# FFN down projection: four pairs of contraction chunks as seven block products, with weight sums made by accumulating DMAs

## The chip, the core and the metric

One core of a Trainium2 chip runs the whole program. The metric is the device time of one execution in microseconds (us), lower is better. Before the change it is 2257.29 us, the median of 3 runs (2256.53 to 2257.57).

## The reference, cut to what matters

Two blocks of two layers each work on x of 256 tokens by 1024 channels in fp32. Every layer has two feed-forward stages (FFN) with a mixing stage between them, so there are eight FFNs:

```python
D_MODEL, SEQ, D_FF, DEPTH = 1024, 256, 2816, 2

def swiglu(h, w1, w3, w2):
    return (jax.nn.silu(h @ w1) * (h @ w3)) @ w2

h = rmsnorm(x, g_ffn1[l])
x = x + 0.5 * swiglu(h, w1_a[l], w3_a[l], w2_a[l])
...
h = rmsnorm(x, g_ffn2[l])
x = x + 0.5 * swiglu(h, w1_b[l], w3_b[l], w2_b[l])
```

The change is in the last product of each FFN, `( ... ) @ w2`: 256 x 2816 times 2816 x 1024.

## The kernel before, in words

**Products.** Each fp32 product is made of three matmuls: every operand is split into a rounded part ("hi", fp32r) and the rest ("lo"), and hi·hi, hi·lo and lo·hi are added in PSUM. Weights come in units of 128 x 2048 elements (1 MB). SP loads a unit in two DMAs into a ring `raw` of RAW = 3 buffers; ACT rounds it into `whi` (`split`, L1176); DVE subtracts to get `wlo` (`split`, L1646) and raises `w_ready`; PE uses both and raises `w_used`. `whi` and `wlo` have HL = 4 slots, so ACT may split unit u once PE is done with unit u - 4, and SP may load unit u once `w_ready` of unit u - 3 is there. All engines run in the order of the program text, and semaphores tie them together.

**One FFN.** It has FC = 22 hidden blocks of 128 channels (b = 0 to 21), one unit each, with gate and up weights side by side. For block b PE runs 16 matmuls of 512 columns and 16 of 256 (`hidden_chunks`, L666 and L667; in the very first FFN `hidden_high` and `hidden_low`, L677 and L685) into one of three pairs of PSUM banks. ACT then copies a part out (`low_parts`, L1242), DVE adds and scales (L1775, L1780), ACT applies silu (L1248), DVE multiplies (`hid`, L1785), ACT rounds `ht_hi` (L1253), and DVE makes `ht_lo` (L1791). In the same round DVE splits unit b + 3 and ACT splits unit b + 4.

**The down projection.** The 22 chunks of 128 hidden channels are the contraction; the result has two token tiles (m = 0, 1) and two halves of 512 channels. Before, 12 units per FFN are used: for half 0 five units of four chunks and one of two, then the same for half 1. `blocks` (L602 to L604) runs, for each chunk and each m, three matmuls of 128x512. After half 0 DVE adds its two PSUM banks to x with the factor `rhalf` (`add_to_x`, L1690), PE transposes that half of x for the next stage (`x_transposes`, L634) early in half 1, ACT and DVE turn it into the next stage's operand (L1188, L1661).

POOL does nothing before but four instructions at the start.

Of the kernel before, what the change touches and what calls it, by code (L numbers as in the profile page):

```python
# [27 lines left out]
P = 128  # L28
T = 256
# [9 lines left out]
SPACER = 40  # L39
RAW = 3  # L40
HL = 4

LAYERS = 2
FFN_UNITS = 2 * FG + 12
# [7 lines left out]
for b in (1, 2):  # L52
    for u in (0, FFN_UNITS + MIX_UNITS[b]):
        SHORT[b].update({u + FFN_UNITS - 7: 1024, u + FFN_UNITS - 1: 1024})
UNITS_BEFORE = {1: 0, 2: LAYERS * LAYER_UNITS[1]}
TOTAL_UNITS = LAYERS * (LAYER_UNITS[1] + LAYER_UNITS[2])
assert all(n % HL == 0 for n in LAYER_UNITS.values())
# [38 lines left out]
class Engine:  # L96
# [50 lines left out]

    def layer(self):

        return {1: 0, 2: LAYERS, "end": 2 * LAYERS}[self.block] + self.lay  # L150

# [24 lines left out]
def build(nc, a, known):  # L176
# [13 lines left out]
    with ctx:  # L190
# [19 lines left out]
        rhalf = sb(ctx, "rhalf", [P, MT])  # L210
        fss = sb(ctx, "fss", [P, 2, 2, MT])
# [32 lines left out]
        junk = sb(ffn, "junk", [P, MT, D])  # L244
        junk2 = sb(ffn, "junk2", [P, MT, D])
        gfin = sb(ffn, "gfin", [P, D])
        xgf = sb(ffn, "xgf", [P, MT, D])
# [116 lines left out]
        stored = semaphore("stored")  # L364

# [10 lines left out]
        def loaded(e, u):  # L376

            return 32 * (e.unit(u) // RAW + 1) - 16
# [28 lines left out]

        block = ctx.enter_context(nc.Block())
# [3 lines left out]
        def _(eng):  # L412
# [5 lines left out]
            def load(u, halves):  # L418

                r = e.unit(u) % RAW  # L420
                eng.wait_ge(w_ready, units(e, u))
                for dst, src in halves:
                    eng.dma_start(dst(raw[:, r, :]), src).then_inc(raw_in[r], 16)
# [29 lines left out]
            def ffn_loads(u0, gate_up_w, w2):  # L453
# [8 lines left out]
                for half in range(2):  # L462
                    for i in range(6):
                        plain(w2, FF, 4 * P * i, 512 * half, u0 + 2 * FG + 6 * half + i, 4 if i < 5 else 2)
# [80 lines left out]
            for _ in e.layers(1):  # L545
                ffn_loads(0, a["t_gate_up_1a"], a["w2_a"])
# [6 lines left out]
                ffn_loads(FFN_UNITS + MIX_UNITS[1], a["t_gate_up_1b"], a["w2_b"])  # L553
            for _ in e.layers(2):
                ffn_loads(0, a["t_gate_up_2a"], a["ffn1_w_down_2"])
# [7 lines left out]
                ffn_loads(FFN_UNITS + MIX_UNITS[2], a["t_gate_up_2b"], a["ffn2_w_down_2"])  # L563
# [15 lines left out]
        def _(eng):  # L579
# [7 lines left out]
            def blocks(u, block, p, split, chunks, start, stop, used, cols=512, beside=False, ready=True):  # L587
# [4 lines left out]
                slot = u % HL  # L592
                if block == 0 and ready:
                    eng.wait_ge(w_ready, units(e, u, RAW))
                for i, c in enumerate(chunks):
                    w = slice((block + i) * cols, (block + i + 1) * cols)
                    out = w if beside else slice(0, cols)
                    first = start and (beside or i == 0)
                    final = stop and (beside or i == len(chunks) - 1)
                    for m in range(MT):  # L600
                        t = slice(m * P, (m + 1) * P)
                        nc.tensor.matmul(pair(p, m)[:, out], hi[:, c, t], whi[:, slot, w], start=first, stop=False)  # L602
# [6 lines left out]
            def last_blocks(u, p, split, chunks):  # L609

                hi, lo = split
                slot = u % HL
# [45 lines left out]
            def hidden_chunks(u, p, chunks):  # L658

                slot = u % HL  # L660
# [11 lines left out]
            def hidden_high(u, p, chunks):  # L672

                for c in chunks:
                    for j in range(2):
                        first = 256 * c + P * j
                        nc.tensor.matmul(pair(p, j), whi[:, u % HL, first:first + P], xt[:, c, :, :], start=c == 0,  # L677
                                         stop=False)

            def hidden_low(u, p, chunks):  # L680

                for c in chunks:
                    for j in range(2):
                        first = 256 * c + P * j
                        last = nc.tensor.matmul(pair(p, j)[:, 0:T], wlo[:, u % HL, first:first + P], xt_hi[:, c, :],  # L685
# [4 lines left out]
            def ffn_tensor(u0, f, next_stage):  # L690
# [76 lines left out]

                u = u0 + 2 * FG
# [5 lines left out]
                blocks(u + 5, 0, 2, HT, (20, 21), False, True, True)  # L774

                u += 6
                blocks(u, 0, 1, HT, (0, 1), True, False, False)
# [3 lines left out]
                blocks(u, 2, 1, HT, (2, 3), False, False, True)  # L781
                for i in range(1, 5):
                    blocks(u + i, 0, 1, HT, range(4 * i, 4 * i + 4), False, False, True)
                if next_stage == "end":
                    last_blocks(u + 5, 1, HT, (20, 21))
                else:
                    blocks(u + 5, 0, 1, HT, (20, 21), False, True, True)
# [377 lines left out]
        def _(eng):  # L1165
            e = Engine(eng, counts, known, act_own)

            def split(u):
# [3 lines left out]
                r = e.unit(u) % RAW  # L1172
# [3 lines left out]
                nc.scalar.activation(whi[:, u % HL, 0:n], raw[:, r, 0:n], ACT.Copy).then_inc(hi_done, 1)  # L1176
# [58 lines left out]
            def ffn_scalar(u0, f, next_stage):  # L1235
                stage = f"ffn{f}"

# [12 lines left out]
                def hidden_hi(b):  # L1250

                    eng.wait_ge(hid_done, ffn_blocks(e, f, b))
                    nc.scalar.activation(ht_hi[:, b, :], hid[:, b % 2, :], ACT.Copy).then_inc(ht_hi_done, 1)  # L1253

# [39 lines left out]
                for b in range(2, FC):  # L1294
# [6 lines left out]
                    split(u0 + b + 4)  # L1301
                for s in range(2 * FG + 1, FFN_UNITS):
                    if s == 2 * FG + 6:
# [8 lines left out]
                    split(u0 + s + 3)  # L1312
# [321 lines left out]

        @block.vector
        def _(eng):
            e = Engine(eng, counts, known, dve_own)

            def split(u):
# [4 lines left out]
                r = e.unit(u) % RAW  # L1644
                n = SHORT.get(e.block, {}).get(u, 2048)
                nc.vector.tensor_tensor(wlo[:, u % HL, 0:n], raw[:, r, 0:n], whi[:, u % HL, 0:n],  # L1646
# [77 lines left out]
            def rstd_diag(stage):  # L1724

                nc.vector.memset(ones[:, :], 1.0)
                nc.vector.tensor_scalar(rhalf[:, :], rstd[:, :], 0.5, None, ALU.mult)
                for m in range(MT):
# [40 lines left out]
            def ffn_vector(u0, f, next_stage):  # L1769
                stage = f"ffn{f}"  # L1770

# [16 lines left out]
                def hidden_lo(b):  # L1788
# [3 lines left out]
                        ht_done, 1)  # L1792

# [41 lines left out]
                for b in range(2, FC):  # L1835
# [6 lines left out]
                    split(u0 + b + 3)  # L1842
                    hidden_lo(b)
                split(u0 + FC + 3)
                for s in range(2 * FG + 1, FFN_UNITS - 1):
                    if s == 2 * FG + 5:
                        multiplied(u0 + s)
# [571 lines left out]
```

## Time and profile before

| what | value |
|---|---|
| median of 3 runs | 2257.29 us |
| profiled execution, first to last instruction (span) | 2255.2 us |
| left around it, by the median | 2.1 us |
| PE busy | 2249.8 us, 100% |
| DVE busy | 1546.0 us, 69% |
| ACT busy | 1238.9 us, 55% |
| POOL busy | 0.2 us |
| mean granted TensorE clock | 1.000 |
| loaded by DMA | 417.61 MB, mean 185 GB/s |

The profile's times are of one execution. Busy time of PE is the union of its matmuls, which overlap (one of 512 columns lasts 0.39 us while the next starts after 0.23 us), so the cost of a matmul is the distance between two starts, not its length.

### The profile page before, as it was taken

The numbers are of one execution on the slowest core, as the hardware profiler recorded it, in microseconds if no ns is written. First come the engines' busy times: TensorE is split into PE (matmuls) and PEld (weight loads), VectorE is DVE, ScalarE is ACT, GpSimd is POOL, SyncE is SP. The second block draws the span as 40 slices with busy tenths as digits, with TensorE's granted clock in tenths as the row PEclk, the third lists the DMA queues.
The fourth block names the chain that finished last, engine by engine and source line by source line (L and its number), as shares of the span: only waits on it lengthen the run. The fifth ranks groups of instructions, "written<-read, shape, count | busy, mean of one in ns | idle before, by whom it ended". The sixth has DMA issues, their size and how long they took to land.

```text
span 2255.2 us, 28960 instructions
## 1 busy us (share of the span) xinstructions
PE 2249.8 (100%) x11686; PEld 1920.7 (85%) x11686; DVE 1546.0 (69%) x2179; ACT 1238.9 (55%) x1489; POOL 0.2 (0%) x4
## 2 busy tenths in 40 slices
PE   9999999999999999999999999999999999999999
PEld 8888888888888888888888888888888888888887
DVE  7764567765774566775776599767657747976773
ACT  7644445554653544654554576465555537755652
POOL 0000000000000000000000000000000000000000
PEclk9999999999999999999999999999999999999999
DMA  7556455555555455554555553545555555345553
GB/s 264 205 198 219 168 191 175 196 196 174 191 187 205 168 175 199 187 197 169 201 190 202 192 169 129 206 155 191 206 177 187 185 180 195 109 172 196 184 191 126
DMA packets 176213, 417.61 MB, mean 185 GB/s; under 512 B 16816, under 2 KB 20784, under 8 KB 176080
## 3 DMA queue, kind: packets, MB, share of 16 engines
q1 hardware_dynamic: 175936, 415.76, 53.3%
q8 instruction: 92, 1.51, 0.3%
q14 instruction: 41, 0.34, 0.0%
q10 hardware_dynamic: 144, 0.00, 0.0%
HBM read 414.66 MB, written 1.05 MB: 184 GB/s over the span
## 4 chain that ended last, share of the span: by engine, by line
PE 98%; DMA 1%; DVE 0%; SPq 0%; ACT 0%; issue 0%; DVEq 0%
PE psum L666 25%; PE psum L602 17%; PE psum L604 17%; PE psum L603 17%; PE psum L667 13%; PE psum L677 3%; PE psum L634 2%; PE psum L685 2%; PE psum L976 1%; DMA xt_in<-t_xt_dram 0%; PE psum L797 0%; DMA raw<-t_gate_up_1a_dram 0%; PE psum L954 0%; PE psum L817 0%; PE psum L944 0%; PE psum L966 0%
## 5 line engine op out<-in xcount | busy, mean ns | idle before, releaser
L1646 DVE TENSOR_TENSOR split_w<-raw,split_w 128x2048 fp32r<-128x2048 f32 (+1 forms) x405 | 881.1, 2182 | 285.8 <-ACT split_w L1176 284.9
L1176 ACT ACTIVATE split_w<-raw 128x2048 fp32r<-128x2048 f32 (+1 forms) x405 | 736.2, 1828 | 311.1 <-PE psum L604 288.2
L666 PE MATMUL psum<-xt,split_w 128*128 128x512 f32 x2464 | 859.2, 393 | 0.1
L667 PE MATMUL psum<-xt,split_w 128*128 128x256 f32 x2464 | 689.2, 280 | 0.0
L666 PEld LDWEIGHTS psum<-xt,split_w 128*128 128x128 f32 x2464 | 461.2, 187 | 104.3 <-DVE split_w L1646 1.3
L667 PEld LDWEIGHTS psum<-xt,split_w 128*128 128x128 f32 x2464 | 465.3, 189 | 0.3
L602 PE MATMUL psum<-split_w,xt 128*128 128x512 f32 (+1 forms) x736 | 289.5, 393 | 0.0
L604 PE MATMUL psum<-split_w,xt 128*128 128x512 f32 (+1 forms) x736 | 283.7, 385 | 0.0
L603 PE MATMUL psum<-split_w,xt 128*128 128x512 f32 (+1 forms) x736 | 283.6, 385 | 0.0
L602 PE MATMUL psum<-split_w,ht_hi 128*128 128x512 f32 x700 | 272.9, 390 | 0.0
L604 PE MATMUL psum<-split_w,ht_lo 128*128 128x512 f32 x700 | 272.5, 389 | 0.0
L603 PE MATMUL psum<-split_w,ht_hi 128*128 128x512 f32 x700 | 272.5, 389 | 0.0
L1775 DVE TENSOR_TENSOR gate<-psum,low 128x256 f32<-128x256 f32 x176 | 74.5, 423 | 155.3 <-ACT low L1242 155.1
L602 PEld LDWEIGHTS psum<-split_w,xt 128*128 128x128 f32 x736 | 138.4, 188 | 28.9 <-issue 3.0
L604 PEld LDWEIGHTS psum<-split_w,xt 128*128 128x128 f32 x736 | 138.2, 188 | 28.1
L1242 ACT ACTIVATE low<-psum 128x512 f32<-128x512 f32 x176 | 104.5, 594 | 103.7 <-PE psum L667 94.3
L603 PEld LDWEIGHTS psum<-split_w,xt 128*128 128x128 f32 x736 | 138.4, 188 | 25.6
L1248 ACT ACTIVATE gate<-gate 128x256 f32<-128x256 f32 x176 | 72.9, 418 | 158.4 <-DVE gate L1780 158.4
L604 PEld LDWEIGHTS psum<-split_w,ht_lo 128*128 128x128 f32 x700 | 131.4, 188 | 27.3
L602 PEld LDWEIGHTS psum<-split_w,ht_hi 128*128 128x128 f32 x700 | 131.4, 188 | 27.2
L603 PEld LDWEIGHTS psum<-split_w,ht_hi 128*128 128x128 f32 x700 | 131.4, 188 | 26.9
L1253 ACT ACTIVATE ht_hi<-hid 128x256 fp32r<-128x256 f32 x176 | 72.6, 417 | 91.4 <-DVE hid L1785 91.4
(278 smaller groups left out, 1951.2 us busy)
## 6 DMA issues: line engine op xcount, KB each, us to landing
raw<-w_in_dram SPq DMA_DIRECT2D x180, 512.0 KB, 4.4
raw<-t_gate_up_1b_dram SPq DMA_DIRECT2D x88, 512.0 KB, 4.1
raw<-t_gate_up_2a_dram SPq DMA_DIRECT2D x88, 512.0 KB, 4.1
raw<-t_gate_up_2b_dram SPq DMA_DIRECT2D x88, 512.0 KB, 4.1
raw<-t_gate_up_1a_dram SPq DMA_DIRECT2D x84, 512.0 KB, 4.1
raw<-ffn_w_down_dram SPq DMA_DIRECT2D x80, 512.0 KB, 4.2
raw<-w_a_dram SPq DMA_DIRECT2D x40, 512.0 KB, 4.4
raw<-w_b_dram SPq DMA_DIRECT2D x40, 512.0 KB, 4.4
```

The lines of the kernel that those rows point to most:

```text
L602: nc.tensor.matmul(pair(p, m)[:, out], hi[:, c, t], whi[:, slot, w], start=first, stop=False)
L603: nc.tensor.matmul(pair(p, m)[:, out], hi[:, c, t], wlo[:, slot, w], start=False, stop=False)
L604: last = nc.tensor.matmul(pair(p, m)[:, out], lo[:, c, t], whi[:, slot, w], start=False, stop=final)
L666: nc.tensor.matmul(bank, whi[:, slot, w], xt[:, c, :, :], start=c == 0, stop=False)
L667: last = nc.tensor.matmul(bank[:, 0:T], wlo[:, slot, w], xt_hi[:, c, :], start=False, stop=c == DC - 1)
L677: nc.tensor.matmul(pair(p, j), whi[:, u % HL, first:first + P], xt[:, c, :, :], start=c == 0, stop=False)
L1176: nc.scalar.activation(whi[:, u % HL, 0:n], raw[:, r, 0:n], ACT.Copy).then_inc(hi_done, 1)
L1242: nc.scalar.activation(low[:, b % 2, :, :], psum[:, first:first + 2, T:2 * T], ACT.Copy).then_inc(low_done, 1)
L1248: nc.scalar.activation(gate[:, b % 2, :], gate[:, b % 2, :], ACT.Silu).then_inc(gate_done, 1)
L1253: nc.scalar.activation(ht_hi[:, b, :], hid[:, b % 2, :], ACT.Copy).then_inc(ht_hi_done, 1)
L1646: nc.vector.tensor_tensor(wlo[:, u % HL, 0:n], raw[:, r, 0:n], whi[:, u % HL, 0:n], ALU.subtract).then_inc(w_ready, 1)
L1775: return nc.vector.tensor_tensor(out[:, b % 2, :], bank[:, 0:T], low[:, b % 2, j, :], ALU.add)
```

## The change: what it does

Of the 22 chunks, 14 stay as they are (`ALONE`). The other eight form four pairs (4, 5), (8, 9), (12, 13), (16, 17). For a pair the result is a 2 x 2 block product: two token tiles by two chunks, times two chunks by two halves. Before, that is 8 block products of 128x128 by 128x512; now it is 7, by a scheme in which some products take sums of activations and sums of weights. Each of the seven products is one unit that holds its four pairs: `11`, `21`, `22` are plain quarters of the weights, loaded through the ring, and `U`, `T3`, `T2`, `T4` are sums of quarters.

- **Weight sums.** Two buffers `added` hold them. SP loads quarter 11 into the first after unit 14 of the hidden blocks and quarter 12 into the second after unit 16. POOL then issues DMAs that add a quarter from DRAM to what the buffer holds: 12 onto the first (U), 22 onto the second (T3), and later, once U is split, 22 onto the first (T2), and once T2 is split, 21 onto the first (T4). Each sum is two DMAs of 512 KB. ACT's split of such a unit waits for its sum.
- **Activation sums.** After blocks 5, 9, 13 and 17 DVE makes four sums of the pair's activations (128x128 each), ACT rounds them (`sums_rounded`, 128x512) and DVE makes their rest (`sums_lo`).
- **PSUM.** Product 11 starts a bank that T2 and later T3 go on adding to; DVE adds this bank to x between (`part_to_x`, with `rhalf` or `minus_half`), and PE waits on `taken` before T2 and before T3. U has a bank of its own, and the bank pair it shares with 11 is that of hidden block 21. The other products go into the banks of the plain chunks.
- **Order.** The 15 units of the down projection run as `DOWN` lists them; the transposes of half 0 of x now come in the middle of unit 12 of 15.
- Buffers are renumbered (`place` counts only units that go through the ring), and `SPACER` goes from 40 to 32.

The core of the diff:

```diff
+QUARTERS = ("11", "21", "22")
+MIXED = range(4, 20, 4)
+ALONE = ((0, 1, 2, 3), (6, 7, 10, 11), (14, 15, 18, 19), (20, 21))
+DOWN = (("plain", 0, ALONE[0]), ("product", "U"), ("product", "11"), ("plain", 0, ALONE[1]), ("product", "21"),
+        ("plain", 0, ALONE[2]), ("product", "T2"), ("product", "22"), ("plain", 0, ALONE[3]), ("plain", 1, ALONE[0]),
+        ("product", "T4"), ("product", "T3"),
+        ("plain", 1, ALONE[1]), ("plain", 1, ALONE[2]), ("plain", 1, ALONE[3]))
+ADDED = {"U": (0, "12"), "T3": (1, "22"), "T2": (0, "22"), "T4": (0, "21")}
...
-FFN_UNITS = 2 * FG + 12
+FFN_UNITS = 2 * FG + len(DOWN)
...
             def ffn_loads(u0, f, gate_up_w, w2):
...
+                    if b == 14:
+                        eng.wait_ge(ht_done, ffn_blocks(e, f, 2))
+                        added_load(w2, 0, "11")
+                    if b == 16:
+                        added_load(w2, 1, "12")
...
+                def product(u, name):
+                    out, start, stop = OUT[name]
+                    resumed = name in ("T2", "T3")
+                    slot = e.unit(u) % HL
+                    eng.wait_ge(w_ready, units(e, u, RAW))
+                    for i in range(4):
+                        hi, lo = LEFT[name](i)
+                        w = slice(i * 512, (i + 1) * 512)
+                        nc.tensor.matmul(out, hi, whi[:, slot, w], start=start and i == 0, stop=False,
+                                         skip_group_check=resumed)
+                        nc.tensor.matmul(out, hi, wlo[:, slot, w], start=False, stop=False, skip_group_check=resumed)
+                        last = nc.tensor.matmul(out, lo, whi[:, slot, w], start=False, stop=stop and i == 3,
+                                                skip_group_check=resumed)
+                    last.then_inc(w_used, 1)
...
-                for i in range(5):
-                    blocks(u + i, 0, 2, HT, range(4 * i, 4 * i + 4), i == 0, False, True)
+                blocks(u, 0, 2, HT, ALONE[0], True, False, True)
+                eng.wait_ge(pair_free, ffn_blocks(e, f, FC - 1))
+                product(u + 1, "U")
+                product(u + 2, "11")
+                blocks(u + 3, 0, 2, HT, ALONE[1], False, False, True)
+                product(u + 4, "21")
+                blocks(u + 5, 0, 2, HT, ALONE[2], False, False, True)
+                eng.wait_ge(taken, 2 * ffns(e, f) + 1)
+                product(u + 6, "T2")
+                product(u + 7, "22")
                 eng.wait_ge(ht_done, ffn_blocks(e, f, FC - 1))
...
+                product(u + 10, "T4")
+                eng.wait_ge(taken, 2 * ffns(e, f) + 2)
+                product(u + 11, "T3")
...
+            def product_split(u, f, name):
+                if name in QUARTERS:
+                    split(u)
+                    return
+                eng.wait_ge(summed_in[name], 32 * (ffns(e, f) + 1))
+                eng.wait_ge(w_used, units(e, u))
+                nc.scalar.activation(whi[:, e.unit(u) % HL, :], added[:, ADDED[name][0], :], ACT.Copy).then_inc(hi_done, 1)
...
+                def sum_of(name):
+                    i, q = ADDED[name]
+                    for j in range(2):
+                        eng.dma_start(added[:, i, 1024 * j:1024 * j + 1024].rearrange("p (k n) -> p k n", k=2),
+                                      quarter(w2, e.lay, q)[:, 2 * j:2 * j + 2, :], accum_op=ALU.add
+                                      ).then_inc(summed_in[name], 16)
+                eng.wait_ge(added_in[0], 32 * n)
+                sum_of("U")
+                eng.wait_ge(added_in[1], 32 * n)
+                eng.wait_ge(summed_in["U"], 32 * n)
+                sum_of("T3")
+                eng.wait_ge(summed_in["T3"], 32 * n)
+                eng.wait_ge(w_ready, units(e, u + 1, RAW))
+                sum_of("T2")
+                eng.wait_ge(summed_in["T2"], 32 * n)
+                eng.wait_ge(w_ready, units(e, u + 6, RAW))
+                sum_of("T4")
...
+                def sums():
+                    both = hid.rearrange("p two (m t) -> p two m t", m=MT)
+                    e.link(nc.vector.tensor_tensor(sa[:, 0, :], both[:, 0, 1, :], both[:, 1, 1, :], ALU.subtract))
+                    nc.vector.tensor_tensor(sa[:, 1, :], both[:, 0, 0, :], both[:, 0, 1, :], ALU.subtract)
+                    e.link(nc.vector.tensor_tensor(sa[:, 2, :], sa[:, 0, :], both[:, 0, 0, :], ALU.subtract))
+                    nc.vector.tensor_tensor(sa[:, 3, :], sa[:, 2, :], both[:, 1, 0, :], ALU.add).then_inc(sums_done, 1)
```

How it moves instructions, at three places. On ACT, at the end of a round of the hidden blocks that closes a pair (here block 5 of the first FFN; `low` opens the round, and the last row splits a weight unit). The change has:

```order
L1362 ACTIVATE low<-psum 128x512 [waits w_used]
L1368 ACTIVATE gate<-gate 128x256 [waits scaled_done]
L1373 ACTIVATE ht_hi<-hid 128x256 [waits hid_done]
L1378 ACTIVATE sa_hi<-sa 128x512 [waits sums_done]
L1286 ACTIVATE split_w<-raw 128x2048 [waits w_used,raw_in1]
```

Before, the same round was `low`, `gate`, `ht_hi` and the split with nothing between. What is new is the row `sa_hi`, which waits for DVE's sums and stands ahead of the split.

On ACT, the splits of the down projection from its unit 3 on. Before:

```order
L1253 ACTIVATE ht_hi<-hid 128x256 [waits hid_done]
L1176 ACTIVATE split_w<-raw 128x2048 [waits w_used,raw_in1]
L1176 ACTIVATE split_w<-raw 128x2048 [waits w_used,raw_in2]
L1176 ACTIVATE split_w<-raw 128x1024 [waits w_used,raw_in0]
```

The change has (`added` is the buffer of sums, and `summed_in_T2` says that its DMAs landed):

```order
L1373 ACTIVATE ht_hi<-hid 128x256 [waits hid_done]
L1286 ACTIVATE split_w<-raw 128x2048 [waits w_used,raw_in0]
L1286 ACTIVATE split_w<-raw 128x2048 [waits w_used,raw_in1]
L1286 ACTIVATE split_w<-raw 128x2048 [waits w_used,raw_in2]
L1295 ACTIVATE split_w<-added 128x2048 [waits w_used,summed_in_T2]
L1286 ACTIVATE split_w<-raw 128x2048 [waits w_used,raw_in0]
L1286 ACTIVATE split_w<-raw 128x1024 [waits w_used,raw_in1]
L1286 ACTIVATE split_w<-raw 128x2048 [waits w_used,raw_in2]
L1295 ACTIVATE split_w<-added 128x2048 [waits w_used,summed_in_T4]
L1295 ACTIVATE split_w<-added 128x2048 [waits w_used,summed_in_T3]
```

The splits of T2, T4 and T3 stand in line with the others, so what is behind them on ACT waits for the sums too.

On DVE, the same stretch of the change (L2007 is `part_to_x`, which takes a bank out of PSUM; `hid` closes block 21):

```order
L1971 TENSOR_TENSOR hid<-up,gate 128x256 [waits gate_done,pair_free]
L1820 TENSOR_TENSOR split_w<-raw,split_w 128x2048 [waits hi_done]
L1977 TENSOR_TENSOR ht_lo<-hid,ht_hi 128x256 [waits ht_hi_done]
L1820 TENSOR_TENSOR split_w<-raw,split_w 128x2048 [waits hi_done] x3
L2007 SCALAR_TENSOR_TENSOR x<-psum,rhalf,x 128x512 [waits w_used]
L2007 SCALAR_TENSOR_TENSOR x<-psum,rhalf,x 128x512 x2
L1830 TENSOR_TENSOR split_w<-added,split_w 128x2048 [waits hi_done]
```

Before, DVE had only splits here until half 0 was complete. Now three `part_to_x` stand ahead of T2's split, which in turn releases POOL's DMAs for T4.

## Rows read from the trace of the kernel before

**Rows 1.** Page: span, busy time of the engines, and the last chain.
```profile
span 2255.2 us, 28960 instructions
PE 2249.8 (100%) x11686; PEld 1920.7 (85%) x11686; DVE 1546.0 (69%) x2179; ACT 1238.9 (55%) x1489; POOL 0.2 (0%) x4
...
PE 98%; DMA 1%; DVE 0%; SPq 0%; ACT 0%; issue 0%; DVEq 0%
```

**Rows 2.** Waits of PE over the whole span: us in total, times, longest.
```profile
PE psum L1153 <- DVE junk L2302: 1.3, 1, 1.3
PE psum L677 <- DVE xt L1677: 0.6, 1, 0.6
PE psum L677 <- ACT split_w L1176: 0.2, 1, 0.2
```

**Rows 3.** PE in order of time, first down projection: start us, length us.
```profile
130.35 0.40 PE L602 MATMUL psum<-split_w,ht_hi 128*128 128x512 f32 x1
...
135.81 0.39 PE L602 MATMUL psum<-split_w,ht_hi 128*128 128x512 f32 x1
...
163.02 1.03 PE L634 MATMUL psum<-ident,x 128*128 128x128 f32 x8
```

**Rows 4.** Groups by shape, 130 to 191 us: busy us, mean ns; idle before.
```profile
L1646 DVE TENSOR_TENSOR split_w<-raw,split_w 128x2048 fp32r<-128x2048 f32 x10 | 22.7, 2288 | 17.3 <-ACT split_w L1176 17.3
L1176 ACT ACTIVATE split_w<-raw 128x2048 fp32r<-128x2048 f32 x10 | 19.1, 1919 | 23.3 <-PE psum L604 23.3
L1646 DVE TENSOR_TENSOR split_w<-raw,split_w 128x1024 fp32r<-128x1024 f32 x2 | 2.5, 1226 | 4.1 <-ACT split_w L1176 4.1
L1690 DVE SCALAR_TENSOR_TENSOR x<-psum,rhalf,x 128x512 f32<-128x512 f32 x2 | 1.4, 748 | 3.9 <-PE psum L604 3.9
```

**Rows 5.** DVE in order of time, one round of the hidden blocks and the last split.
```profile
114.48 0.42 DVE L1775 TENSOR_TENSOR gate<-psum,low 128x256 f32<-128x256 f32 x1 [1.17 <-ACT low L1242]
114.94 0.42 DVE L1780 TENSOR_TENSOR gate<-gate,rstd_row 128x256 f32<-128x256 f32 x1
115.28 0.41 DVE L1775 TENSOR_TENSOR up<-psum,low 128x256 f32<-128x256 f32 x1
115.92 0.43 DVE L1785 TENSOR_TENSOR hid<-up,gate 128x256 f32<-128x256 f32 x1 [0.22 <-ACT gate L1248]
116.26 2.28 DVE L1646 TENSOR_TENSOR split_w<-raw,split_w 128x2048 fp32r<-128x2048 f32 x1
118.46 0.42 DVE L1791 TENSOR_TENSOR ht_lo<-hid,ht_hi 128x256 fp32r<-128x256 f32 x1
...
133.32 2.28 DVE L1646 TENSOR_TENSOR split_w<-raw,split_w 128x2048 fp32r<-128x2048 f32 x1
```

**Rows 6.** ACT in order of time: dense rounds early, then waiting ones.
```profile
45.89 0.58 ACT L1242 ACTIVATE low<-psum 128x512 f32<-128x512 f32 x1
50.53 0.57 ACT L1242 ACTIVATE low<-psum 128x512 f32<-128x512 f32 x1
...
113.85 0.60 ACT L1242 ACTIVATE low<-psum 128x512 f32<-128x512 f32 x1 [0.81 <-PE psum L685]
...
119.41 0.60 ACT L1242 ACTIVATE low<-psum 128x512 f32<-128x512 f32 x1 [0.81 <-PE psum L685]
...
130.55 0.60 ACT L1242 ACTIVATE low<-psum 128x512 f32<-128x512 f32 x1 [0.81 <-PE psum L685]
```

**Rows 7.** DMA, 130 to 191 us: queue (share), issues (KB, us to landing).
```profile
q1 hardware_dynamic: 7095, 13.81, 65.4%
raw<-w_a_dram SPq DMA_DIRECT2D x12, 512.0 KB, 4.5
```

**Rows 8.** DMA in 40 slices of 130 to 191 us: busy tenths, GB/s.
```profile
DMA  4960648999980039707920089997999992197149
GB/s 107 345 240 0 187 157 242 398 357 351 367 320 30 0 73 345 281 0 200 391 102 0 0 282 271 336 325 243 387 383 406 359 345 70 35 314 266 73 105 399
```

**Rows 9.** Clock over the whole span.
```profile
core 0: 2255.2 us, clock 1.000
```

More of the change, by code:

```diff
@@ L461, in ffn_loads @@
                                   ).then_inc(gfin_in, 16)
-                for half in range(2):
-                    for i in range(6):
-                        plain(w2, FF, 4 * P * i, 512 * half, u0 + 2 * FG + 6 * half + i, 4 if i < 5 else 2)
+                for i, part in enumerate(DOWN):
+                    if part[0] == "plain":
+                        _, half, chunks = part
+                        alone(w2, chunks, 512 * half, u0 + 2 * FG + i)
+                    elif part[1] in QUARTERS:
+                        rows = quarter(w2, e.lay, part[1])
+                        load(u0 + 2 * FG + i, [(chunked(1024 * j, 2, 512), rows[:, 2 * j:2 * j + 2, :]) for j in range(2)])
             def mix1_loads(u0):
@@ L676, in hidden_high @@
                         first = 256 * c + P * j
-                        nc.tensor.matmul(pair(p, j), whi[:, u % HL, first:first + P], xt[:, c, :, :], start=c == 0,
+                        nc.tensor.matmul(pair(p, j), whi[:, e.unit(u) % HL, first:first + P], xt[:, c, :, :], start=c == 0,
                                          stop=False)
@@ L684, in hidden_low @@
                         first = 256 * c + P * j
-                        last = nc.tensor.matmul(pair(p, j)[:, 0:T], wlo[:, u % HL, first:first + P], xt_hi[:, c, :],
+                        last = nc.tensor.matmul(pair(p, j)[:, 0:T], wlo[:, e.unit(u) % HL, first:first + P], xt_hi[:, c, :],
                                                 start=False, stop=c == DC - 1)
@@ L1236, in ffn_scalar @@
                 stage = f"ffn{f}"
+                second = range(MIXED.start + 1, MIXED.stop + 1, MIXED.step)
                 def low_parts(b):
@@ L1770, in ffn_vector @@
                 stage = f"ffn{f}"
+                second = range(MIXED.start + 1, MIXED.stop + 1, MIXED.step)
                 def summed(out, b, j):
@@ new lines, in ffn_vector @@
+                    if b in second:
+                        eng.wait_ge(hid_done, ffn_blocks(e, f, b))
+                        sums()
+                    hidden_lo(b)
+                    if b in second:
+                        sums_lo(second.index(b))
+                down_split(3)
+                EACH, BOTH = psum[:, 0, :], psum[:, 1, :]
+                down_split(4)
+                down_split(5)
+                multiplied(u0 + 2 * FG + 2)
+                for m in range(MT):
+                    part_to_x(m, 1, BOTH, rhalf)
@@ new lines, in ffn_vector @@
+                multiplied(u0 + 2 * FG + 10)
+                e.link(add_to_x(2, 0, hidden=True))
+                multiplied(u0 + 2 * FG + 11)
+                last = part_to_x(1, 0, EACH, rhalf)
+                if next_stage == "end":
+                    last.then_inc(out_ready, MT)
+                else:
+                    last.then_inc(done, e.mark(done, ("x", next_stage, 0)))
+                e.link(part_to_x(1, 1, EACH, minus_half))
+                down_split(14)
+                if next_stage != "end":
+                    x_lo(next_stage, 0)
+                    if next_stage == "ffn0":
+                        half_done()
+                        if (e.block, e.lay) == (1, LAYERS - 1):
+                            eng.wait_ge(gfin_in, 16)
+                            x_scaled(0)
```

208 lines of the change are left out of this document (155 added, 53 removed).

## The prediction

> **What bounds the kernel now.** I read the page first. PE is busy 2249.8 of 2255.2 us and 98% of the chain that ended last is PE; DVE has 69%, ACT 55%, POOL nothing [rows 1]. Then the waits of PE: three, 2.1 us in all, the last two of them while the first weights arrive [rows 2]. So in steady state PE never waits, and time can go only by taking matmuls away or making them shorter. The clock is 1.000 throughout [rows 9], the upper of its two levels (2.4 GHz), so no time is to be had there. Hence two questions: how much PE work goes, and does PE, which now waits for nothing, begin to wait.
>
> **What goes.** From the first down matmul at 130.35 to the transposes at 163.02 there are 132 + 12 = 144 matmuls: (163.02 - 130.35) / 144 = 0.2269 us each [rows 3]. The first 24 agree: 5.46 us [rows 3]. An FFN's down projection has 22 x 2 x 2 x 3 = 264 of them before, and 14 x 2 x 2 x 3 + 7 x 4 x 3 = 252 after. That is 12 less, in eight FFNs 96, and the order of PE is indeed 96 rows shorter. The shapes are the same, and the matmuls of a product are three to an operand as before, so I keep 0.2269: **-21.8 us**. All of it is on the path.
>
> **The activation sums.** A round of a hidden block takes PE 119.41 - 113.85 = 5.57 us; ACT and DVE need only 50.53 - 45.89 = 4.64 us when they are behind, and otherwise wait 0.81 us for PE [rows 6]. In four rounds DVE adds four subtractions of 128 columns, two of them linked to the next by a wait. One of 256 columns takes 0.42 us [rows 5], and 1024 more columns 2.29 - 1.23 = 1.06 us [rows 4], so one of 128 is about 0.29, and the four 1.2 us. They follow the split, which ends at 118.54 [rows 5]; ACT then needs 0.6 us for its 512 columns (`low`, as wide, takes 0.60) [rows 6], and only then starts its split of 1.8 us. The next `low` comes at about 122.0 instead of 119.41: 2.6 us late. Each ordinary round gives 5.57 - 4.64 = 0.93 us back, three of them 2.8, so the delay doesn't grow from pair to pair. PE would notice it when the weights of block b + 3 are late: they are ready at 118.54, and that block starts two blocks after 113.65, at 124.8: 6.2 us of cover. In the first FFN ACT is already 45.89 - (130.55 - 16 x 5.57) = 4.4 us behind at block 5 [rows 6], and would be 7.0 behind after it; but there PE wants the low part only in the last third of a block, 3.7 us later, so the cover is 9.9. I take **0** for this; if all four delays added up, 10.4 - 6.2 = 4.2 us per FFN (a rival below).
>
> **U's bank.** U and 11 use the banks of hidden block 21. DVE frees them 115.69 - 113.85 = 1.84 us after `low` [rows 5, 6], at 132.4, and U starts 5.46 us into the projection, at 135.8: 3.4 us of cover. In the first FFN the delay left over is 4.4 + 4 x 2.6 - 12 x 0.93 = 3.6: about 0.2 us, once.
>
> **Three more splits per FFN.** 15 units instead of 12: 3 x (1.92 + 2.29) us more on ACT and DVE [rows 4], and DVE adds eight banks of 128x512 at 0.75 to x, instead of two, before half 0 is done. DVE waits for ACT 17.3 + 4.1 us of these 61 [rows 4], and the new work fits beside 252 x 0.2269 = 57.2 us of PE. **0** as long as the sums of weights are on time. The transposes of half 0 come 46.3 us into the projection, when PE has 11 us left; the operand needs some 3. At the change from the first block to the second ACT also has squares to do there, and the first units of the next stage may be late: **+1 us**, once (bounds 0 and 3).
>
> **The sums of weights** decide the rest. Let X be the time from POOL's release to the landing of one sum (two DMAs of 512 KB), and t count from the start of the projection. U and T3 are added during the hidden blocks, tens of us ahead. T2's sum is released by U's split, DVE's last but one of the hidden rounds, one round before 133.32 + 2.28: t = 0 [rows 5]. T2 is used at t = 108 x 0.2269 = 24.5; ACT and DVE need 1.92 + 2.29 + 0.1 = 4.3, so X up to 20.2 is free. T4's sum is released by T2's split on DVE. That one stands behind the split of unit 5 (loaded once unit 2 is split, at t = 5.3; landed some 5 later; split by 14.5) and three `part_to_x` (16.6): ready at 18.9. T4 is used at t = 168 x 0.2269 = 38.1, so its sum must be there at 33.8, and X up to 14.9 is free if T2 was on time. If X is over 14.6, T2's own sum makes T2 late (ready at X + 4.3), and the two add: **wait per FFN = 2X - 29.5**, from X = 14.75 on. At X = 16.1 it is 2.7 us and the gain is gone.
>
> The trace has no accumulating DMA and none from POOL. Nearest rows: a plain load of 512 KB lands 4.5 us after its issue with its twin beside it [rows 7], and where all 16 engines are full they move 340 to 406 GB/s [rows 8], so 1 MB is 2.6 to 3.1 us of full engines. Lower end: X = 4.9, as two plain loads. Upper end: every DMA twice as long, since it reads two things, and the halves in series: 4 x 4.5 = 18. Between: the bytes twice, 4.9 + 2.6 = 7.5, and behind the two loads that fall in T4's window (units 12 and 13, 2 MB, 5.2 us): 12.7. The engines are 65.4% busy here already [rows 7], so I take the value with the loads in front: X = 12.7, 2 us inside the limit, cost **0**.
>
> The engines' double reading is also the Trainium skill's rule (Collectives: The Full Stack, section The bandwidth ceiling): an add in the DMA path takes two source reads and runs at half the rate of a copy. No row here shows one. With its figure for 1 MB from POOL's queue (DMA: Bandwidth & Descriptors, section Bandwidth: 6.15 us, and some 2.0 fixed), X would by estimate be 14.3 alone, which still costs 0, and 19.5 behind both loads, a wait of 9.5 us per FFN and a time of 2312.
>
> **Sum.** 2255.2 - 21.8 + 1.2 = 2234.6 for the span; the median of the runs stands 2.1 above it (2257.29), so **2236.7 us**.
>
> **The rivals.**
> - *T4 a little late* (X 14.75 to 15.8): up to 2.1 us per FFN, 2237 to 2253. For it: only 2 us of cover, from a price that I had to build. Against: POOL has nothing else to do.
> - *The sums eat the gain* (X 15.8 to 16.3): 2253 to 2262, no change that can be told. About 0.2%, 4.5 us, is what a measurement of this kernel can tell from no change.
> - *The sums are slow* (X over 16.3): the place is the wait of ACT's T4 split on its sum, with all later splits behind it; PE waits at T4 and perhaps at T2. At X = 18 the wait is 6.5 us, eight times 52: 2289; at X = 20, 84: 2321. It decides from X = 16.1. For it: the busy engines [rows 7], and slices of full ones one after the other where loads bunch [rows 8]; against: it needs each step three to four times as long as a plain load's. Here the skill's rule weighs in (DMA: Bandwidth & Descriptors, section Issuing engines are not separate DMA queues): POOL's DMAs share the 16 engines with SP's. That leaves the order of sum and loads open.
> - *The hidden rounds fall behind*: ACT and DVE don't catch up between pairs and PE waits 4.2 us in seven FFNs: 2266. Against it: 0.93 us a round [rows 6].
> - That it doesn't remove what it says is excluded by the order.
>
> **How the numbers follow.** On time 0.50; T4 a little late 0.19; gain eaten 0.06; sums slow 0.21; rounds behind 0.04. Faster 0.69, same 0.06, slower 0.25. The forecast is the likeliest case, 2236.7, with its own range of 2233 (no edge, and PE's last waits go) to 2241. The range that should hold 8 in 10 goes from 2233 through the next two cases to 2266, the place where X = 16.6 or falling rounds end.
>
> **What would show it.** Right: PE's matmuls 96 fewer and 0.227 us apart, PE still waiting only some 2 us, ACT's splits from `added` released by PE rather than by a DMA, and the issues onto `added` landing in under 14 us. Wrong: waits of PE on DVE's split of `added` at T4 or T2, with ACT's split behind a DMA; or waits at the first blocks after a pair. If X is small and the time is still high, look for slower loads into `raw`, which share the engines.

## The result, and the profile after

The changed kernel takes **2266.92 us** (median of 4 runs, 2261.88 to 2268.88) against 2256.97 (2256.53 to 2257.57) beside it: a ratio of 1.0040, 95% interval 1.0026 to 1.0054. It is slower by about 10 us where I had forecast 2236.7, and it lies just outside my range of 2233 to 2266.

The page after the change: span, busy times, the DMA queues (packets, MB, share of 16 engines) and the last chain, against [rows 1].

```profile
span 2267.0 us, 29248 instructions
PE 2240.8 (99%) x11590; PEld 1907.7 (84%) x11590; DVE 1685.2 (74%) x2419; ACT 1289.5 (57%) x1545; POOL 78.2 (3%) x68
...
q1 hardware_dynamic: 180288, 424.15, 54.8%
q0 software_dynamic: 17408, 33.56, 8.6%
...
PE 67%; DVE 10%; ACT 9%; DMA 8%; issue 5%; POOL 1%; SPq 0%; DVEq 0%; POOLq 0%; ACTq 0%
```

The 96 matmuls are gone, but PE's busy time fell by 9.0 us and not by 21.8, and its idle time rose from 5.4 (2255.2 - 2249.8) to 26.2 us. So the span's + 11.8 is - 21.8 of matmuls that are gone, + 12.8 of longer work on those that stay and + 20.8 of waiting. In the chain, DVE, ACT, DMA and "issue" (mostly POOL's: idle time in which it waited for nothing that the profile shows) now hold a third where PE held 98%. The waits of PE name the place (us in total, times, longest), where [rows 2] had three small ones:

```profile
PE psum L860 <- DVE split_w L1830: 16.6, 6, 5.1
PE psum L701 <- DVE x L2007: 2.1, 3, 0.7
```

L860 is the first matmul of a product, L1830 DVE's split of a sum in `added`. Which product it is stands in the first FFN's rows: POOL's two late sums, T2's and T4's, two DMAs each; then ACT's splits of them; then PE (start, length, idle before and its releaser).

```profile
135.97 1.21 POOL L1785 DMA_DIRECT2D added<-w_a_dram  x1 [30.12 <-DVE split_w L1830]
141.84 1.22 POOL L1785 DMA_DIRECT2D added<-w_a_dram  x1 [4.66 <-issue]
155.12 1.21 POOL L1785 DMA_DIRECT2D added<-w_a_dram  x1 [12.06 <-DVE split_w L1830]
161.28 1.22 POOL L1785 DMA_DIRECT2D added<-w_a_dram  x1 [4.95 <-issue]
...
150.27 1.92 ACT L1295 ACTIVATE split_w<-added 128x2048 fp32r<-128x2048 f32 x1 [2.96 <-DMA added<-w_a_dram]
...
170.80 3.71 ACT L1295 ACTIVATE split_w<-added 128x2048 fp32r<-128x2048 f32 x2 [12.12 <-DMA added<-w_a_dram]
...
175.09 0.79 PE L860 MATMUL psum<-split_w,ht_hi 128*128 128x512 f32 x1 [4.83 <-DVE split_w L1830]
175.68 0.63 PE L862 MATMUL psum<-split_w,ht_hi 128*128 128x512 f32 x1
176.11 0.63 PE L863 MATMUL psum<-split_w,ht_lo 128*128 128x512 f32 x1
```

T2's sum is released at 135.97 and split at 150.27, so X is 14.3 or a little less; PE does not notice it. T4's is released at 155.12 and split at 170.80: X = 15.7, ACT idle for 12.12 us because of it, and PE for 4.83. Then PE goes on at a step of 0.43 us (175.68 to 176.11) instead of the 0.227 of [rows 3]. The windows (length, PE busy, granted clock, DMA share, GB/s) show why; [rows 9] had 1.000 throughout:

```profile
165.00:170.00 5.00, 5.00 (x24) 1.00 1.07 255
170.00:175.00 5.00, 0.26 (x2) 0.92 0.78 300
175.00:180.00 5.00, 4.91 (x12) 0.50 0.00 0
180.00:185.00 5.00, 5.00 (x21) 0.90 0.70 238
```

The clock is at its lower level (1.2 GHz) for some 6 us behind the wait: 0.50 to 180, and 0.90 in the mean of the next 5 us.

T4 in all eight FFNs, read in the same way (t from the first matmul of the projection; "by the steps" is release + X + 4.3 for ACT and DVE - 38.1 for T4's place, as in the prediction):

| FFN | T4's sum released at t | X | wait by the steps | wait measured |
|---|---|---|---|---|
| 1 | 23.8 | 15.7 | 5.7 | 4.83 |
| 2 | 19.9 | 14.2 | 0.3 | none |
| 3 | 20.2 | 15.8 | 2.2 | 1.97 |
| 4 | 18.9 | 15.1 | 0.2 | none |
| 5 | 20.9 | 15.6 | 2.7 | 2.52 |
| 6 | 22.3 | 16.9 | 5.4 | 5.13 |
| 7 | 19.2 | 15.3 | 0.7 | 0.56 |
| 8 | 20.1 | 15.5 | 1.8 | 1.61 |

The geometry of the prediction holds to within 0.9 us; the X that I put into it did not. T2's sums are as slow (13.2 to 16.5 us): the last chain runs through both late sums in six of the eight FFNs and through T4's alone in the fourth and seventh, so a late T2 also moves T4's release.

### The profile page after: what moved, and what is told of

The parts are those of the page before. It is cut to its first block, busy times and chain, and to the rows that moved or that the text cites. A ratio compares the mean times of both kernels' runs of the same rounds, so it can differ in the third digit from the quotient of the medians.

```text
span 2267.0 us, 29248 instructions
## 1 busy us (share of the span) xinstructions
PE 2240.8 (99%) x11590; PEld 1907.7 (84%) x11590; DVE 1685.2 (74%) x2419; ACT 1289.5 (57%) x1545; POOL 78.2 (3%) x68
## 4 chain that ended last, share of the span: by engine, by line
PE 67%; DVE 10%; ACT 9%; DMA 8%; issue 5%; POOL 1%; SPq 0%; DVEq 0%; POOLq 0%; ACTq 0%
PE psum L733 17%; PE psum L669 11%; PE psum L671 11%; PE psum L670 11%; PE psum L734 9%; ACT split_w L1286 4%; DMA added<-ffn_w_down_dram 3%; DVE split_w L1820 3%; DVE split_w L1830 2%; PE psum L701 2%; ACT split_w L1295 2%; DMA added<-w_a_dram 2%; ACT low L1362 1%; DVE gate L1966 1%; DVE hid L1971 1%
## 5 line engine op out<-in xcount | busy, mean ns | idle before, releaser
L1820 DVE TENSOR_TENSOR split_w<-raw,split_w 128x2048 fp32r<-128x2048 f32 (+2 forms) x397 | 861.9, 2180 | 175.2 <-ACT split_w L1286 173.3
L1286 ACT ACTIVATE split_w<-raw 128x2048 fp32r<-128x2048 f32 (+2 forms) x397 | 719.3, 1825 | 169.6 <-PE psum L671 117.2
L669 PE MATMUL psum<-split_w,ht_hi 128*128 128x512 f32 x444 | 173.4, 390 | 0.0
L671 PE MATMUL psum<-split_w,ht_lo 128*128 128x512 f32 x444 | 172.9, 389 | 0.0
L670 PE MATMUL psum<-split_w,ht_hi 128*128 128x512 f32 x444 | 172.9, 389 | 0.0
L1830 DVE TENSOR_TENSOR split_w<-added,split_w 128x2048 fp32r<-128x2048 f32 x32 | 73.2, 2287 | 80.3 <-ACT split_w L1295 80.3
L1295 ACT ACTIVATE split_w<-added 128x2048 fp32r<-128x2048 f32 x32 | 60.3, 1908 | 101.4 <-DMA added<-ffn_w_down_dram 53.6
L1971 DVE TENSOR_TENSOR hid<-up,gate 128x256 f32<-128x256 f32 x176 | 74.1, 425 | 36.9 <-ACT gate L1368 35.8
```

Of the source, the lines that this page charges most:

```text
L670: nc.tensor.matmul(pair(p, m)[:, out], hi[:, c, t], wlo[:, slot, w], start=False, stop=False)
L671: last = nc.tensor.matmul(pair(p, m)[:, out], lo[:, c, t], whi[:, slot, w], start=False, stop=final)
L1286: nc.scalar.activation(whi[:, e.unit(u) % HL, 0:n], raw[:, r, 0:n], ACT.Copy).then_inc(hi_done, 1)
L1295: nc.scalar.activation(whi[:, e.unit(u) % HL, :], added[:, ADDED[name][0], :], ACT.Copy).then_inc(hi_done, 1)
L1820: nc.vector.tensor_tensor(wlo[:, e.unit(u) % HL, 0:n], raw[:, r, 0:n], whi[:, e.unit(u) % HL, 0:n], ALU.subtract).then_inc(w_ready, 1)
L1830: nc.vector.tensor_tensor(wlo[:, slot, :], added[:, ADDED[name][0], :], whi[:, slot, :], ALU.subtract).then_inc(w_ready, 1)
```

## The experiments

Three theories of X = 14 to 17 us. **A**: the space for POOL's descriptors holds one DMA of the two, so the second waits for the first (each second DMA has 4.6 to 8.7 us of "issue" ahead of it). **B**: the sums share the engines with the loads of weights. **C**, which came later: an adding DMA is slow by itself. And is the sum's lateness the whole loss?

**1. Without the late sums.** ACT doesn't wait for T2's and T4's sums and POOL doesn't issue them (these two products multiply what lies in `added`).

```diff
-                eng.wait_ge(summed_in[name], 32 * (ffns(e, f) + 1))
+                if name in ("U", "T3"):
+                    eng.wait_ge(summed_in[name], 32 * (ffns(e, f) + 1))
...
-                sum_of("T2")
...
-                sum_of("T4")
```

> The two late sums are left out: POOL adds nothing for T2 and T4, and their splits read the buffer as U's sum left it, so two of the seven products have wrong weights. If the late sums (and the half clock after PE's waits for them) are the whole loss: no wait of PE on a split of added, clock 1.000, PE busy 21 to 23 us under before, 2234 to 2239 us. If something else costs time too (activation sums, more splits, slower loads into raw): over 2245 us, with waits of PE at other places.

Measured: 2236.45 us (2236.31 to 2239.01), ratio 0.9909 (0.9895 to 0.9924). The page's busy times:

```profile
PE 2228.0 (100%) x11590; PEld 1902.2 (85%) x11590; DVE 1686.8 (75%) x2419; ACT 1292.9 (58%) x1545; POOL 39.3 (2%) x36
```

and PE's longest waits:

```profile
PE psum L744 <- ACT split_w L1286: 1.5, 1, 1.5
PE psum L1263 <- DVE junk L2544: 1.3, 1, 1.3
```

PE's busy time is 21.8 us below [rows 1], to the tenth what 96 x 0.2269 gives. The activation sums, the three more splits and the eight banks added to x cost next to nothing (PE's idle time is 6.7 us, 1.3 more than before). The late sums are the whole loss, 30.5 us.

**2. Twice the descriptor space.**

```diff
-dynamic_dma_scratch_size=1024
+dynamic_dma_scratch_size=2048
```

> Descriptor space of POOL's DMAs doubled, 1024 to 2048 bytes a partition, nothing else. Theory A (a sum is slow because POOL holds its second DMA until the first has drained from that space, 4.6 to 5.4 us): the idle time before the second DMA goes to under 0.5 us, T4's sum lands 10 to 12 us after its release instead of 14 to 16, PE's waits on T4 go, 2235 to 2241 us. Theory B (a sum is slow because SP's loads fill the engines): the second DMA is issued early but lands as late as before, 14 us or more after the release, and the time stays at 2255 to 2267 us.

Measured: 2255.93 us (2254.18 to 2258.94), ratio 0.9994 (0.9985 to 1.0003). POOL now issues both DMAs of a sum in one go (2.46 us for two, no "issue" ahead of the second), and T4's sum in the first FFN takes 12.1 us (157.87 to 169.97). Waits for T4 fall from 16.6 to 6.9 us, none over 2.0. So A is a part, 3.6 us of X in that FFN, and not the whole; X fits what A had said (10 to 12), the time does not (2235 to 2241). In the mean of the eight FFNs X falls from 15.5 to 12.1, but T4's release moves from t = 20.7 to 22.9 (here 25.4): with both DMAs of a sum out at once, loads of weights land later (in the second FFN that of unit 5 at t = 12.5 instead of 9.9), and ACT and DVE split behind them. So a good part of what the sum gains is lost by the loads.

**3 and 4. T4 later.** In the second half of the projection T3 and a plain unit change places with T4, which gives its sum 8.2 us more; x's first half is then finished one unit later. The second run has the larger descriptor space as well.

```diff
-        ("product", "T4"), ("product", "T3"),
-        ("plain", 1, ALONE[1]), ("plain", 1, ALONE[2]), ("plain", 1, ALONE[3]))
+        ("product", "T3"), ("plain", 1, ALONE[1]), ("product", "T4"),
+        ("plain", 1, ALONE[2]), ("plain", 1, ALONE[3]))
...
-HALF_LAST = 11
+HALF_LAST = 12
...
```

> T4 moves behind the first four chunks of half 1, T3 ahead of it: 36 matmuls, 8.2 us, more for T4's sum; x's half 0 is complete 8.2 us later. The longest wait of PE at T4 was 5.1 us, so both theories expect the waits on T4 to go, the clock back at 1.000, and 2235 to 2241 us. If the late completion of half 0 costs time at the next stage instead: waits of PE at the transposes or at the next stage's first units, 2245 us or more.

> Both edits of the two runs before together. Theory A: waits gone with room to spare, 2234 to 2239 us, equal to the run without late sums within 3 us. Theory B: as the run with T4 moved alone.

Measured: 2246.11 us (2245.54 to 2247.27), ratio 0.9950 (0.9935 to 0.9965), and 2248.33 (2245.35 to 2249.21), ratio 0.9957 (0.9940 to 0.9973). No wait for T4 is left in either, so the space adds nothing where the sum has time. What PE waits for instead stands at the start of the next FFN, at three of the boundaries:

```profile
PE psum L733 <- DVE split_w L1820: 6.6, 3, 3.7
```

**5. The sums alone.** At the end of the program, behind the stores, POOL issues four transfers with nothing beside them: plain 512 KB, adding 512 KB, a plain pair, an adding pair, each waited for.

```diff
+            eng.wait_ge(stored, 64)
...
+            for n, (whole, how) in enumerate(((1, {}), (1, {"accum_op": ALU.add}), (2, {}), (2, {"accum_op": ALU.add}))):
+                for j in range(whole):
+                    eng.dma_start(added[:, 0, 1024 * j:1024 * j + 1024].rearrange("p (k n) -> p k n", k=2),
+                                  rows[:, 2 * j:2 * j + 2, :], **how).then_inc(alone[n], 16)
+                eng.wait_ge(alone[n], 16 * whole)
```

> POOL waits for the four stores at the end and then issues, with nothing else on the queues, a plain 512 KB load, an accumulating one, a plain pair and an accumulating pair (two of 512 KB); only their rows count, the total grows by their length. Theory A (descriptor space holds the second DMA of a pair): in both pairs POOL sits in issue idle of 4 to 9 us ahead of the second DMA, and a pair takes over 1.5 times one. Theory B (in the down projection the sums share the engines with the loads of weights): an accumulating pair alone takes well under the 14.2 to 16.9 us that it took there, 7 to 10 us. Theory C (an accumulating DMA is slow by itself): the accumulating pair takes 13 us or more alone, and the plain one clearly less, 6 to 8 us.

Measured (2293.76 us in one run, with the four transfers): POOL's rows, each row's start being the landing of the transfer ahead of it; the span ends at 2291.9.

```profile
2262.51 0.76 POOL L1812 DMA_DIRECT2D added<-w_a_dram  x1 [35.23 <-DMA out_dram<-x]
2266.92 1.20 POOL L1812 DMA_DIRECT2D added<-w_a_dram  x1 [3.65 <-DMA added<-w_a_dram]
2272.91 1.50 POOL L1812 DMA_DIRECT2D added<-w_a_dram  x2 [4.80 <-DMA added<-w_a_dram]
2279.82 1.22 POOL L1812 DMA_DIRECT2D added<-w_a_dram  x1 [5.40 <-DMA added<-w_a_dram]
2285.70 1.23 POOL L1812 DMA_DIRECT2D added<-w_a_dram  x1 [4.66 <-issue]
```

Plain 4.4 us, adding 6.0, plain pair 6.9, adding pair 12.1. The plain pair goes out at once (x2), the adding one in two steps 5.9 us apart, as long as the first one takes. The 12.1 lie between what B (7 to 10) and C (13 or more) had said: 12.1 of the 14.2 to 16.9 us are there with nothing else on the engines, which leaves B 2.1 to 4.8.

**6. Plain loads in place of the late sums.** The same bytes from DRAM, by POOL, at the same places, without the addition, so that T2 and T4 multiply other weights.

```diff
+                    how = {"accum_op": ALU.add} if name in ("U", "T3") else {}
...
-quarter(w2, e.lay, q)[:, 2 * j:2 * j + 2, :], accum_op=ALU.add
+quarter(w2, e.lay, q)[:, 2 * j:2 * j + 2, :], **how
```

> The sums of T2 and T4 become plain loads: the same bytes from DRAM by the same engine and at the same places, without the addition (so T2 and T4 multiply other weights). Theory C (adding is what takes the time): release to landing falls from 14.2 to 16.9 us to 8 to 11, PE's waits for T4 go, 2237 to 2242 us. Theories A and B (issuing, or sharing with the loads): 13 to 16 us as before, waits for T4 stay, 2255 to 2267 us.

Measured: 2237.12 us (2236.72 to 2238.64), ratio 0.9911 (0.9898 to 0.9925), no waits for T4. X for T4 in the first FFN is 163.69 - 157.04 = 6.65 us, among all the loads. The queue of POOL in 131 to 191 us (packets, MB, share of 16 engines) and its issues (KB, median us to landing), of the changed kernel:

```profile
q0 software_dynamic: 1088, 2.10, 20.1%
...
added<-w_a_dram POOLq DMA_DIRECT2D x4, 512.0 KB, 7.1
```

and of this run:

```profile
q0 software_dynamic: 576, 2.10, 11.7%
...
added<-w_a_dram POOLq DMA_DIRECT2D x4, 512.0 KB, 5.3
```

For the same bytes the adding DMAs take 272 packets each instead of 144, and 0.201 x 60 = 12.1 us of all 16 engines instead of 7.0. C it is, with A behind it: the plain pair goes out at once and the adding pair does not. That it is the packets that fill the descriptor space fits both, but no run varies their number alone.

**7. The boundary put right.** Experiment 3 with the splits of the FFN's last two units ahead of the work on x.

```diff
-HALF_LAST = 12
+HALF_LAST = 13
...
                 down_split(14)
+                down_split(15)
                 if next_stage != "end":
                     x_lo(next_stage, 0)
...
-                down_split(15)
                 down_split(16)
```

> T4 late as in the run with the late T4 (2246.1 us), and at the end of each FFN the splits of the last two units stand ahead of the work on x (ScalarE rounds the turned x behind the split of the first unit of the next stage, VectorE subtracts for the last unit of the FFN ahead of its own part). If the 6.6 us of PE waits at three boundaries and the half clock behind them come from that order: the split that PE waited for is done 2 us sooner, 2237 to 2241 us. If they come from the loads being late there: 2244 to 2248 us, with the wait now on a DMA's account. If the half-row of x is now late in its place: over 2248.

Measured: 2241.62 us (2240.24 to 2243.36), ratio 0.9929 (0.9916 to 0.9943): faster than both kernels. The waits there are fewer, not gone, and the longest stands at the change from the first block to the second:

```profile
PE psum L733 <- DVE split_w L1820: 4.3, 2, 3.1
```

**8 and 10. A wait without a transfer.** Experiment 1, and ACT makes T4's split four times, or six times, more ahead of the one that counts.

```diff
+                for _ in range(4 if name == "T4" else 0):
+                    e.link(nc.scalar.activation(whi[:, e.unit(u) % HL, :], added[:, ADDED[name][0], :], ACT.Copy))
```

> No late sums (as in the run that left them out, 2236.45 us), and ScalarE makes T4's split four times more ahead of the one that counts: about 8 us of delay, of which 3.4 us are slack, so PE waits some 4.3 us in each of the 8 FFNs, with no transfer to blame. If a wait costs its length alone: 2236.5 + 8 x 4.3 = 2271 us and PE busy stays 2228. If the granted clock drops to half behind it as behind the waits for the sums (some 2.7 us each): about 2292 us, PE busy about 2250, and windows at 0.50 behind each wait.

> As the run with the delayed ScalarE, with six split copies more instead of four: 11.6 us of delay against a slack of 6.4 (that run waited 1.25 us in each FFN with four copies, at a granted clock of 1.00), so PE waits about 5.1 us at T4 in each FFN, as long as the longest waits for a sum. If the clock falls behind a wait of that length whatever caused it: windows near 0.50 behind each wait, PE busy some 2250 us, about 2305 us in all. If the half clock belonged to the transfers: granted clock 1.00, PE busy about 2234, 2285 to 2290 us.

With four: 2258.34 us (2257.25 to 2260.36). I had taken T3's row for T4's: the slack is 6.4 us, so PE waited only 1.25 us at T4, and the run could not answer. It told something else, that the clock stays up behind this wait (PE's first row behind it):

```profile
171.59 0.50 PE L860 MATMUL psum<-split_w,ht_hi 128*128 128x512 f32 x1 [1.25 <-DVE split_w L1827]
```

and the windows around it, with columns as above:

```profile
170.00:175.00 5.00, 3.66 (x15) 1.00 0.00 0
175.00:180.00 5.00, 5.00 (x23) 1.00 0.40 120
```

With six: 2296.66 us (2296.18 to 2300.98), between the two times that I had named, so the clock has to decide. PE waits for T4 as long as for the two latest sums (4.83 and 5.13), here 5.14 us up to 174.33 in the first FFN and, in the view of the waits, in all:

```profile
PE psum L860 <- DVE split_w L1827: 41.1, 8, 5.1
```

The windows around the first of these waits:

```profile
170.00:175.00 5.00, 0.67 (x2) 0.63 0.00 0
175.00:180.00 5.00, 5.00 (x17) 0.68 0.00 0
180.00:185.00 5.00, 5.00 (x27) 1.00 0.87 294
```

The DMA share is 0.00 during and just behind the wait, and the clock still falls. PE's busy time is 2247.8, or 19.8 more than in experiment 1: 2.5 us for each of eight waits. With 39.9 us more of idle time (41.1 at T4, 1.2 less elsewhere) that is the 59.7 us by which the span is longer. So a wait of 5 us cost 7.5 here, with no transfer beside it.

**9. Alone, with twice the descriptor space.** Experiments 2 and 5 together.

> The same four transfers alone at the end, with the descriptor space doubled to 2048 bytes. With 1024 bytes the plain pair took 6.9 us, the accumulating single 6.0 and the accumulating pair 12.1, its second DMA issued 5.9 us behind the first. Theory A (the space makes one wait for the other): the second is issued some 1.2 us behind the first and the accumulating pair takes 7 to 9 us, near the plain pair. Theory C (the addition itself runs at that rate): both are issued at once and the pair still takes 11 to 12 us.

Measured (2283.39 us in one run; the span ends at 2281.6), POOL's rows again:

```profile
2260.37 1.20 POOL L1812 DMA_DIRECT2D added<-w_a_dram  x1 [3.63 <-DMA added<-w_a_dram]
2266.39 1.50 POOL L1812 DMA_DIRECT2D added<-w_a_dram  x2 [4.83 <-DMA added<-w_a_dram]
2272.50 2.46 POOL L1812 DMA_DIRECT2D added<-w_a_dram  x2 [4.61 <-DMA added<-w_a_dram]
```

and a window inside the adding pair (length, busy times of the five engines, granted clock, DMA share, GB/s):

```profile
2275.00:2278.00 3.00, 0.00 (x0) 0.00 (x0) 0.00 (x0) 0.00 (x0) 0.00 (x0) 0.50 1.05 186
```

The plain pair takes 6.1 us and the adding pair 9.1, between what A and C had said. While it runs, the engines are full at 186 GB/s, where the fullest slices of [rows 8] had plain loads at 271 to 406. So of the 12.1 us alone, 6 are a plain pair, 3 the addition and 3 the space for descriptors. In the first FFN's stage the same three steps are 6.65 (experiment 6), 12.1 (experiment 2) and 15.7 (the change): addition 5.5, space 3.6. The addition costs more there than alone. Experiment 2's trace shows that the rest is B: the queues of POOL and SP in the first FFN (packets, MB, share of 16 engines), first from T2's release to its landing (137.24 to 146.16), then from T4's (157.87 to 169.96):

```profile
q0 software_dynamic: 544, 1.05, 72.2%
q1 hardware_dynamic: 210, 0.42, 12.4%
...
q0 software_dynamic: 544, 1.05, 51.7%
q1 hardware_dynamic: 707, 1.38, 35.8%
```

The sums take 6.4 and 6.3 us of all 16 engines; the loads beside them take 1.1 and 4.3, and X is 8.9 and 12.1. In all eight FFNs T2's sums take 8.4 to 9.2 us, as long as the 9.1 alone, and T4's 11.6 to 12.6. So the loads beside T4's sum cost it some 3 us.

## Why the prediction was wrong

- **What goes, - 21.8 us**: right. Experiment 1 shows it in PE's busy time.
- **The activation sums, 0**: right, and by its steps. DVE's four subtractions take 1.14 us and ACT's rounding 0.63, ACT waiting 2.84 us for them:

```profile
117.52 0.28 DVE L1983 TENSOR_TENSOR sa<-hid 128x128 f32<-128x128 f32 x1
...
118.37 0.29 DVE L1986 TENSOR_TENSOR sa<-sa,hid 128x128 f32<-128x128 f32 x1
...
118.70 0.63 ACT L1378 ACTIVATE sa_hi<-sa 128x512 fp32r<-128x512 f32 x1 [2.84 <-DVE sa L1986]
```

  There is no wait of PE behind a pair of blocks. **U's bank**: 0.2 us once forecast, 0.2 measured (L860 behind `up`). But the lag left over in the first FFN, which I counted only there, also moves the release of T2's sum: it comes 4.6 us into the projection and not at t = 0 (0.7 to 1.3 in the other seven). That lag is why T4's release stands at t = 23.8 there, against 18.9 in my steps and 18.9 to 22.3 elsewhere.
- **Three more splits, 0, and the boundary, + 1**: right in size, in part by luck. Experiment 1 with both stands at 2236.45 where the sum gave 2236.7, but the change of blocks costs PE 0.5 us there; the other wait that is new, 1.5 us where [rows 2] had 0.2, is among the first hidden blocks (at 24.6 us), where I had counted none.
- **The sums of weights, X = 12.7, cost 0**: this is the step that failed. X is 14.2 to 16.9 us, 15.5 in the mean of the eight, and the limit that I had worked out, 14.9, is passed in seven of them. The value was built as a plain pair (4.9) with the bytes twice (2.6) behind two loads (5.2). What was missing is that the two DMAs of a sum don't overlap: the second goes out when the first is done, 5.9 us later alone and 6.2 at T4 in the first FFN. With the larger space, where it goes out at once, X is 12.1 in the mean, so this is 3.4 of the 15.5. My upper end had just that ("the halves in series"), and I took the lower value because of the 65.4% of busy engines [rows 7], which say nothing on how POOL issues. That the 12.7 stands near 12.1 is in part luck: the pair (6.1) and the addition (3.0 alone) cost more than I took, the loads (some 3) less. (My 340 to 406 GB/s left out the slower of the full slices, from 271 on.)
- **T4's release at t = 18.9**: not safe either. In experiment 2 X is inside the limit of 14.9 in all eight FFNs, and PE still waits 6.9 us for T4, because the release comes at 21.1 to 25.4. I had split unit 5 by 14.5, as if the sums left its load alone; the slower loads into `raw` stood in the prediction as a sign only.
- **The price of a wait**: I let a wait cost its own length. It costs the length and, behind the longer ones, a stretch at half clock: PE's matmuls took 12.8 us more, beside 20.8 of idle time. Of the 12.8, 8.9 are the clock: behind the waits in the first, third, fifth and sixth FFN 17.9 us of PE's work ran at 0.50. (For the rest see the last section, on experiment 8.) So break-even was not at X = 16.1. With the formula, X = 15.5 gives 1.5 us per FFN, 12 us, and 2249: the rival "T4 a little late". The measured 2267 is that rival's mechanism at a higher price: late sums are spread (14.2 to 16.9, releases at 18.9 to 23.8), so the waits for T4 make 16.6 us instead of 12, and the 12.8 come on top.

The Trainium skill (Collectives: The Full Stack, section The bandwidth ceiling) has a ReduceScatter, whose add needs two source reads, at about half the rate of an AllGather's copy. The traces come near it: 7.0 / 12.1 = 0.58 by engine time in the stage, and alone, in experiment 5, the pairs take 3.1 and 6.5 us of all 16 engines, 0.48. The estimates that I had made from the Trainium skill's figure for 1 MB from POOL's queue (DMA: Bandwidth & Descriptors, section Bandwidth), X = 14.3 alone and 19.5 behind both loads, are not borne out: the runs show 12.1 or 9.1 alone, by the descriptor space, and 14.2 to 16.9 in the stage. The measurements decide.

## What to carry to other kernels

An adding DMA is no load with an addition for free: price it by the engine time of its packets and by whether two of them fit into the descriptor space, and look at "issue" ahead of a second DMA on the issuing engine. Where it must be just in time, move its consumer later rather than its transport faster: one unit's swap gave 21 us, twice the descriptor space 11, since the faster sum made the loads beside it late, and both together no more than the swap. And a wait of 5 us on TensorE cost 7.5 here, so a margin of 2 us on a price that no row shows is none.

## What was not expected of the hardware

- A plain DMA of 512 KB from POOL takes 144 packets, an adding one 272; with 1024 bytes of descriptor space two of the first go out together and two of the second don't (4.6 to 8.7 us of idle time ahead of the second), with 2048 both do.
- The granted clock falls to its lower level behind waits of 5 us with no DMA running (experiment 10), and stays at the upper one behind waits of 1.25 us (experiment 8). In the changed kernel it was at 0.50 for 3.4 us behind the waits of 1.97 and 2.52 us, and stayed at 1.00 behind that of 1.61.
- In experiment 8 PE's busy time still grew by 6.3 us at a clock of 1.000. Counted from start to start against experiment 1, T4's first two steps come 1.5 us later for 1.25 of idle time, the first two of T3 0.3 for 0.1, and the first transpose 0.87 for 0.72 in seven FFNs: some 21 of the 22.3 us of span. A matmul of 0.39 us overlaps the next, which starts 0.23 behind it; ahead of a wait that overlap of 0.16 is lost, and the step behind the first matmul is 0.35 instead of 0.23.
